# Neighbourhood attention inside a hybrid block: from one grid row of queries to tiles of 4 rows by 16 columns, with key spans of 32 columns

## The chip, the cores and the metric

The kernel runs on one core of one Trainium2 chip. The metric is the device time of one execution in microseconds. Three runs of the kernel before took 4218.52, 4212.82 and 4217.05 us; their median, 4217.05 us, is the time before.

## The reference

The program is a chain of blocks: a first block with three branches (neighbourhood attention, gated linear attention, RWKV), an output projection, windowed attention, mixture of experts, a linear recurrence and mixture of experts again. Only the neighbourhood attention of the first block changes. It works on 16 meta tokens and a grid of 16 rows by 64 columns of tokens, in 8 heads of 64. Each query sees the 16 meta tokens and a window of 8 rows by 16 columns, clipped at the grid's border, with a bias by the relative position:

```python
def row_block(r):
    rs = jnp.clip(r - wr // 2, 0, rows - wr)          # wr = 8
    kw = kb[:, :, :, col_idx]                         # 16 columns for each query column
    s_loc = jnp.einsum('bhcd,bhrckd->bhcrk', qr, kw) * scale + bias
    s_meta = jnp.einsum('bhcd,bhmd->bhcm', qr, km_h) * scale
    p = jax.nn.softmax(jnp.concatenate([s_loc, s_meta], axis=-1), axis=-1)
    return p_loc @ vw + p_meta @ vm_h                 # the result is gated by silu(g)
```

## The kernel before, in words

The attention branch is one stage between two barriers of all engines. It goes over four pairs of heads (`p` = 0 to 3; two heads of 64 fill 128 partitions). For each pair TensorE projects V, K, Q and the gate G from the normed input `hnT` (1088 columns), eight matmuls (`project_tensor`, L409) to each span of 336, 384, 320 or 512 columns, into banks 6 and 7 in turn. ScalarE copies each span out (`span_scalar`, L508 and L511). V is then turned by 16 transposes in four groups (`turn_tensor`, L422 and L425), and ScalarE copies each group (`turn_scalar`, L516 and L519).

V, K and Q of the first pair and three of the gates are projected ahead. After that a loop takes 64 items, one for each pair and each grid row `r`, in a software pipeline written out by hand. In iteration `i` TensorE issues the values matmuls of item `i-3`, half of the fill, the transposes of item `i-2`, the other half of the fill, and the scores of item `i`. The fill is the projection of the next pair's V, K and Q: 4 matmuls in each iteration, 2 in each half. In the last pair it is one matmul of the last gate in each iteration.

One item is 64 queries of two heads, 128 partitions in all:

- Scores (L456, L458): the window of 8 whole grid rows, 512 keys, and 16 meta keys in a second bank. For each head one matmul with 64 rows and 64 columns of the array.
- VectorE: meta scores scaled (L605), their maximum (L607), scores plus bias and mask with their maximum (L609), the negative (L614), and later the reciprocal of the sum (L595) and the probabilities scaled by it (L597). The keys outside the 16 columns are masked with -1e30.
- ScalarE: Exp with the sum (L561).
- TensorE: four transposes of 128 keys and one of 16 (L465, L466). ScalarE copies the four (L555), VectorE the fifth (L601).
- TensorE: values (L476, L478), five matmuls for each head. VectorE multiplies the result by the gate into `oT` (L589; in the last pair a plain copy, L591).

Three items are under way at once, each with two banks: `scores_tensor` waits for `o_taken` of the item three before. The bias comes by 8 DMAs on SyncE's queue (L359), and one VectorE instruction (L575) scales it and adds the mask that GpSimd builds. GpSimd also clears a corner of a weight buffer for the next stage (L324) once V of the last pair is projected. SyncE's queue holds the weight blocks, the bias after the fourth block, and the stores of `oT`.

A float32 matmul is two records of LDWEIGHTS and two of MATMUL in the trace; a transpose is one of each.

Of the kernel before, what the change touches and what calls it, by code (L numbers as in the profile page):

```python
# [13 lines left out]
P = 128  # L14
# [251 lines left out]
def attention_branch(k, c, ps, io, hnT, mix, sb):  # L266
# [6 lines left out]
    with stage(k, sb) as st:  # L273
        NP, NR, RING = BW // P, SEQ // CH, 4
        n = NP * NR
        wb = k.first + [st.sb(f"w_block{i}", [P, KD, P]) for i in range(2, RING)]
        ahead, low = [t.now() for t in k.first_in], st.sem("gla_low_cleared")
        qT, kT = [st.sb(f"na_q{x}", [P, SEQ]) for x in range(2)], [st.sb(f"na_k{x}", [P, COLS]) for x in range(2)]
        vT, vt = st.sb("na_v", [P, COLS]), [st.sb(f"na_v_tiles{x}", [P, NC, P]) for x in range(2)]
        gate = st.sb("na_gate", [P, NP, SEQ])  # L280
        bias = st.sb("na_bias", [P, NP * RPB_R, CH])
        away, edge = st.sb("na_outside", [P, CH]), st.sb("na_edge", [P, 2, CH])
# [4 lines left out]
        g, bias_in, biased = st.sem("na_setup"), st.sem("na_bias_in"), st.sem("na_biased")  # L287
        w_in = [st.sem(f"na_w_in{i}") for i in range(RING)]
# [4 lines left out]
        p_turned, p_copied, pm_copied, pv, o_taken, finished = (st.sem(name) for name in (  # L293
            "p_turned", "p_copied", "pm_copied", "pv", "o_taken", "finished"))
# [12 lines left out]
        turns_before = lambda s: 4 * sum(s > at[K, p][1] for p in range(NP))  # L307
# [5 lines left out]
        def turn_bank(p, i):  # L313
            return ps[6 + (at[K, p][1] + 1 + 4 * p + i) % 2]

        def spans_done(b):

            kind, p = blocks[b]
            return at[kind, p][1] + len(span_of[kind])

# [5 lines left out]
        def setup_gpsimd(gp):  # L326
            def select(ap, fill, base, pattern, part):
                gp.wait_ge(*g.now())
                gp.affine_select(out=ap, in_=ap, compare_op=ALU.is_ge, fill=fill, base=base, pattern=pattern,
                                 channel_multiplier=part).then_inc(*g.up())  # L330

            for h in HALF:
                gp.wait_ge(*g.now())
                gp.memset(away[h, :], 0.0).then_inc(*g.up())
                for base, col, q in ((WIN_C // 2, 1, -1), (WIN_C // 2 - 1, -1, 1)):
                    select(away[h, :], NEG, base + (CH - 1) * q, [[col, CH]], -q)
                for e, (base, q) in enumerate(((WIN_C // 2 - 1, -1), (-(CH - WIN_C // 2), 1))):
                    gp.wait_ge(*g.now())
                    gp.memset(edge[h, e, :], 1.0).then_inc(*g.up())
                    select(edge[h, e, :], 0.0, base + (CH - 1) * q, [[0, CH]], -q)  # L340
                    select(edge[h, e, :], 0.0, (WIN_C - 1) if e == 0 else -(CH - WIN_C),
                           [[-1 if e == 0 else 1, CH]], 0)
            gp.wait_ge(*g.now())
            gp.tensor_tensor(edge[:, 0, :], edge[:, 0, :], edge[:, 1, :], ALU.add).then_inc(*g.up())
            gp.wait_ge(*g.now())
            gp.tensor_scalar(edge[:, 0, :], edge[:, 0, :], -1.0, 1.0, ALU.mult, ALU.add).then_inc(*g.up())
            gp.wait_ge(*g.now())
            gp.tensor_tensor(away[:, :], away[:, :], edge[:, 0, :], ALU.mult).then_inc(*g.up())

        def window(r):  # L350
            first = min(max(r - WIN_R // 2, 0), NC - WIN_R)
            return first, first - r + WIN_R - 1

        def load_bias(sp):
            rpb = bass.AP(io["rpb_padded"].tensor, RPB_PAD + WIN_C - 1 - (CH - 1),
                          [[RPB_R * RPB_C, BW // 64], [1, CH], [RPB_C, RPB_R], [1, CH]])
            for h in range(2):
                for p in range(NP):
                    sp.dma_start(bias[HALF[h], p * RPB_R:(p + 1) * RPB_R, :], rpb[2 * p + h]).then_inc(*bias_in.up(16))  # L359

        def store(sp, p):
            if p < NP - 1:
                sp.wait_ge(o_taken.sem, NR * (p + 1))
# [23 lines left out]
        def span_free(pe, s):  # L387

            for p in range(NP):
                i = s - at[K, p][1] - 1  # L390
                if 0 <= i < 2:
                    pe.wait_ge(vcopied.sem, 5 * p + (3, 5)[i])
                    return
            if s >= 2:
                pe.wait_ge(copied.sem, s - 1)
# [18 lines left out]
        def turn_tensor(pe, p, i):  # L414

            pe.wait_ge(copied.sem, at[V, p][1] + 3)
            if i < 2:
                pe.wait_ge(copied.sem, at[K, p][1] + i)
            else:
                pe.wait_ge(vcopied.sem, 5 * p + i - 1)  # L420
            for j in range(4 * i, min(4 * i + 4, NC - 1)):
                x = pe.transpose(turn_bank(p, i)[:, (j % 4) * P:(j % 4 + 1) * P], vT[:, X0 + CH * j:X0 + CH * j + P],  # L422
                                 c["ident"][:, :])
            if i == 3:
                x = pe.transpose(turn_bank(p, i)[0:META, 3 * P:], vT[:, M0:X0], c["ident"][:, :])  # L425
            x.then_inc(*vturned.up())

        def fill_tensor(pe, p, r, part):

# [3448 lines left out]
```

## Time and profile before

| | us |
|---|---|
| median of 3 runs | 4217.05 |
| the profiled execution's own time | 4214.0 |
| its span | 4212.3 |
| mean granted TensorE clock, share of full | 0.979 |
| the attention stage's first matmul to the next stage's first matmul, from the timeline | 30.07 to 446.89 |
| its loop's first scores to its last ones | 119.96 to 432.57 |

Time between the stage's two ends is time of the whole kernel, since barriers of all engines stand on both sides. TensorE's busy time in the profile is a sum of records whose ends are modelled; where work follows work, the distance between two starts is the better measure.

### The profile page before, as it was taken

Reading aid. Unit: us, or ns where it says so; the run is one execution under the profiler, and the core shown is the slowest. Engines: PE = TensorE matmul, PEld = TensorE weight load, DVE = VectorE, ACT = ScalarE, POOL = GpSimd, SP = SyncE. Lnnn points to the kernel's source line nnn. Section 1 sums busy time; section 2 is a strip of 40 time slices with the busy share of each in tenths; the row PEclk is TensorE's granted clock in tenths of the full one; section 3 lists DMA queues with packets and bytes.
Section 4 is the critical chain, followed back from the end, with each engine's and each line's share of the span. In section 5 each row is a group of like instructions: output and inputs, shape, how many; then the busy total and the mean of one; then the engine's idle time right before and its main releaser. Section 6 shows DMA issues by size and latency. Waiting matters only on the chain. (4 is left out here: it accounts for less than half of the span.)

```text
span 4212.3 us, 65895 instructions
## 1 busy us (share of the span) xinstructions
PE 4009.1 (95%) x28648; PEld 2243.9 (53%) x28648; DVE 1549.1 (37%) x3413; ACT 1058.6 (25%) x2123; POOL 270.7 (6%) x342
## 2 busy tenths in 40 slices
PE   8999999999999989999998999999899998999998
PEld 4555675586868664554544444444444454444443
DVE  2344233445454541124657311111455649111113
ACT  2333221343334320104552000001245321000003
POOL 0000000101111100000110000000000100000000
PEclk9999999999999999999998999999999998999999
DMA  3000101100000013221008899999311129899997
GB/s 100 26 26 7 51 17 41 31 4 26 4 27 9 17 46 108 63 40 31 1 1 320 295 329 308 328 313 312 127 34 45 50 103 328 297 319 319 314 323 247
DMA packets 315088, 566.97 MB, mean 135 GB/s; under 512 B 48001, under 2 KB 121889, under 8 KB 314801
## 3 DMA queue, kind: packets, MB, share of 16 engines
q1 hardware_dynamic: 299328, 505.61, 35.1%
q0 software_dynamic: 9504, 34.61, 3.4%
q10 hardware_dynamic: 5968, 22.55, 1.4%
q8 instruction: 226, 3.70, 0.4%
q14 instruction: 62, 0.50, 0.0%
HBM read 514.46 MB, written 48.23 MB: 134 GB/s over the span
## 5 line engine op out<-in xcount | busy, mean ns | idle before, releaser
L3364 PE MATMUL bank<-ring,m_picked_T 128*128 128x512 f32 x2048 | 897.1, 596 | 4.1 <-ACT m_picked_T L3447 4.1
L3364 PEld LDWEIGHTS bank<-ring,m_picked_T 128*128 128x128 f32 x2048 | 388.9, 191 | 481.3 <-issue 475.7
L3364 PE MATMUL bank<-ring,m_hidden_T 128*128 128x512 f32 x1024 | 455.1, 592 | 0.0
L3364 PEld LDWEIGHTS bank<-ring,m_hidden_T 128*128 128x128 f32 x1024 | 189.7, 190 | 215.3 <-issue 215.2
L3613 DVE TENSOR_TENSOR m_hidden<-m_hidden,bank 128x512 f32<-128x512 f32 x64 | 43.9, 685 | 505.1 <-ACT m_hidden L3453 505.1
L1450 PE MATMUL bank<-hnT,first_block 128*128 128x336 f32 (+3 forms) x544 | 180.4, 483 | 8.5 <-PEq L101 7.8
L3453 ACT ACTIVATE m_hidden<-bank 128x512 f32<-128x512 f32 x64 | 38.2, 597 | 538.8 <-PE bank L3364 538.8
L241 PE MATMUL bank<-xT,first_block 128*128 128x512 f32 x352 | 152.4, 593 | 2.8 <-ACT l_i L3092 1.7
L2648 PE MATMUL bank<-xT,a_weights 128*128 128x512 f32 x320 | 142.3, 595 | 0.8 <-ACT xT L2504 0.8
L1450 PEld LDWEIGHTS bank<-hnT,first_block 128*128 128x128 f32 x544 | 102.1, 193 | 67.5 <-issue 21.2
L2728 PE MATMUL bank<-a_weights,xT 128*128 128x512 f32 x256 | 126.7, 622 | 5.0 <-DMA a_weights<-in_attn_w_o 4.6
L3619 DVE COPY m_hidden_T<-bank 128x256 f32<-128x256 f32 x64 | 27.0, 422 | 276.1 <-PE bank L3357 276.1
L409 PE MATMUL bank<-hnT,first_block 128*128 128x512 f32 (+3 forms) x336 | 123.0, 507 | 1.4 <-PEq L101 1.4
L409 PE MATMUL bank<-hnT,w_block 128*128 128x512 f32 (+3 forms) x304 | 124.3, 536 | 0.0
L3457 ACT ACTIVATE m_hidden_T<-bank 128x256 f32<-128x256 f32 x64 | 24.5, 383 | 393.5 <-PE bank L3357 393.5
L3743 POOL DMA_INDIRECT y_rows<-m_ys,m_tokens x30 | 47.7, 1589 | 1113.3 <-DVE m_ys L3628 1046.3
L2101 DVE TENSOR_TENSOR rw_lane<-bank,rw_lane 128x512 f32<-128x512 f32 (+1 forms) x100 | 60.9, 609 | 145.6 <-PE bank L1632 145.6
L241 PEld LDWEIGHTS bank<-xT,first_block 128*128 128x128 f32 x352 | 66.6, 190 | 87.3 <-issue 86.1
L3044 PE MATMUL bank<-xT,l_gT 128*128 128x512 f32 x256 | 110.1, 592 | 0.8 <-ACT l_i L3092 0.8
L3030 PE MATMUL bank<-l_xc,l_wg 128*128 128x512 f32 x256 | 110.5, 592 | 0.0
L1632 PE MATMUL bank<-rw_lane 64*64 64x64 f32 x2720 | 100.7, 218 | 5.3 <-issue 5.2
L1615 PE MATMUL bank<-rw_lane 64*64 64x64 f32 x2720 | 100.3, 220 | 3.9 <-issue 2.9
(500 smaller groups left out, 6091.5 us busy)
## 6 DMA issues: line engine op xcount, KB each, us to landing
ring<-in_moe_w_gate_up SPq DMA_DIRECT2D x512, 512.0 KB, 7.6
ring<-in_moe_w_down SPq DMA_DIRECT2D x256, 512.0 KB, 4.6
first_block<-in_w_in SPq DMA_DIRECT2D x23, 512.0 KB, 3.7
w_block<-in_w_in SPq DMA_DIRECT2D x19, 512.0 KB, 3.7
x_rows<-X ACTq DMA_DIRECT2D x2, 4096.0 KB, 17.5
ring<-y_rows SPq DMA_DIRECT2D x16, 512.0 KB, 8.9
out_w<-in_w_out ACTq DMA_DIRECT2D x11, 512.0 KB, 13.6
first_block<-in_lru_w_in SPq DMA_DIRECT2D x11, 512.0 KB, 3.9
```

Source lines behind the costliest of these rows:

```text
L241: m = pe.matmul(ps[banks + j][0:out_rows, 0:n], w[:, d, 0:out_rows], src[:, d, col:col + n], start=d == 0, stop=d == KD - 1)
L409: x = pe.matmul(bank_of(s + j)[:, 0:w], wb[b % RING][:, d, :], hnT[:, d, col:col + w], start=d == 0, stop=d == KD - 1)
L1450: m = pe.matmul(banks[j][:, 0:n], wb[i % 3][:, d, :], hnT[:, d, col:col + n], start=d == 0, stop=d == KD - 1)
L1615: x = pe.matmul(L.tall(0)[B_(d), h, i, :], power_t(L, e, d, h, i), power(L, e, d, h, i))
L1632: x = pe.matmul(L.tall(2)[B_(d), h, i, :], power(L, e, d, h, i), L.TT[B_(d), h, i, :])
L2101: ve.tensor_tensor(L.part(2), L.bank[2][:, 0:2 * L.n * CH], L.part(2), ALU.add).then_inc(*tt_added.up())
L2648: x = pe.matmul(main_bank(s)[:, :], w, xT[:, d, tokens_of(s)], start=d == 0, stop=d == KD - 1)
L2728: x = pe.matmul(ps[6 + half][:, :], oT[:, b, t * P:(t + 1) * P], weights[:, b, 512 * half:512 * half + 512], start=b == 0, stop=b == KD - 1)
L3030: out = pe.matmul(ps[s % 4][:, :], wg[:, q, z, h, x * P:(x + 1) * P], xc[:, h, col:col + w], start=h == 0, stop=h == 1)
L3044: out = pe.matmul(ps[2 * (t % 4) + h][:, :], gT[:, b, t * P:(t + 1) * P], wo[:, b, 512 * h:512 * h + 512], start=b == 0, stop=b == KD - 1)
L3364: m = pe.matmul(banks[j][:, :], lhsT[:, (i % 8) * P:(i % 8 + 1) * P], ring[:, i, j, :], start=i % 8 == 0, stop=i % 8 == KD - 1)
L3743: gp.indirect_dma_start(y_rows[:, :], bass.IndirectOffsetOnAxis(ap=tokens[:, e:e + 1], axis=0), ys[:, :], None, compute_op=ALU.add).then_i ...
```

## The change

An item is now a tile of 4 grid rows by 16 columns of queries, still 64 queries of two heads, and there are still 16 of them to a pair of heads. Its keys are a span of 32 columns (from column 0, 8, 24 or 32) of 9, 12, 12 or 10 lines, with the meta tokens in one of these lines: 288, 384, 384 or 320 keys in a single bank. Items are handled two at a time, so that the loop has 32 steps; a step's half of the fill is four matmuls (one in the last pair). The bias arrives as 12 by 48 values for each query, by 32 DMAs of 16 partitions. GpSimd cuts twelve "images" from it for each pair (bias plus mask, for three kinds of tile and four row blocks) during the loop. The masks are built on 32 partitions, turned by four transposes in bank 0 and copied by VectorE. V is kept four times, once for each column window, which makes five groups of four transposes. Queries are stored tile by tile.

```diff
-        s_sb, pT, stat = ([st.sb(f"na_{name}{u}", shape) for u in range(3)] for name, shape in (
-            ("scores", [P, 512 + META]), ("probs_T", [P, 5, P]), ("stats", [P, 6])))
+        FIRST, LONG, META_LINE = (0, 0, 4, 8), (9, 12, 12, 10), (4, 4, 0, 9)
+        vT, vt = st.sb("na_v", [P, 4, V_LINES, WIDE]), [st.sb(f"na_v_tiles{x}", [P, 4, 5, P]) for x in range(2)]
+        s_sb = [st.sb(f"na_scores{u}", [P, 3 * P]) for u in range(6)]
+        pT = [st.sb(f"na_probs_T{u}", [P, 3, P]) for u in range(6)]
...
+        def images_gpsimd(gp):
+            gp.wait_ge(mask_in.sem, 1)
+            gp.wait_ge(biased.sem, 1)
+            for p, rb in ((p, rb) for p in range(NP) for rb in range(4)):
+                if p:
+                    gp.wait_ge(maxed.sem, STEPS * (p - 1) + 2 * rb + 2)
...
+                    for x in range(3):
+                        for line, row, count in ROWS[rb]:
+                            gp.tensor_tensor(image[f][rb][:, x, line:line + count, :], rows[...],
+                                             mask[:, x, :].unsqueeze(1).broadcast_to([P, count, WIDE]), ALU.add)
...
-            for h in HALF:
-                pe.matmul(a[h, :], qT[p % 2][h, CH * r:CH * r + CH], kT[p % 2][h, first:first + 512])
-            for h in HALF:
-                x = pe.matmul(b[h, 0:META], qT[p % 2][h, CH * r:CH * r + CH], kT[p % 2][h, M0:X0])
+            if t >= 3:
+                pe.wait_ge(o_taken.sem, 2 * (t - 2))
+            for i in (2 * t, 2 * t + 1):
+                for h in range(2):
+                    x = pe.matmul(bank(i)[half(i, h), 0:LONG[rb] * WIDE].rearrange("p (r c) -> p r c", c=WIDE),
+                                  qT[p % 2][HALF[h], queries], lines(kT[p % 2], FIRST[rb], LONG[rb], w)[HALF[h]])
...
-            for j in range(4):
-                pe.transpose(a[:, j * P:(j + 1) * P], s_sb[u][:, j * P:(j + 1) * P], c["ident"][:, :])
-            pe.transpose(b[0:META, P:2 * P], s_sb[u][:, 512:512 + META], c["ident"][:, :]).then_inc(*p_turned.up())
+            for j in range(3):
+                keys = P if j < 2 else tail(rb)
+                x = pe.transpose(bank(i)[0:keys, j * P:(j + 1) * P], s_sb[i % 6][:, j * P:j * P + keys], c["ident"][:, :])
...
+            for j in range(3):
+                keys = P if j < 2 else tail(rb)
+                for h in range(2):
+                    x = pe.matmul(bank(i)[HALF[h], 3 * P:3 * P + CH], vt[p % 2][0:keys, w, FIRST[rb] // 4 + j, HALF[h]],
+                                  pT[i % 6][0:keys, j, half(i, h)], start=j == 0, stop=j == 2)
...
+            for t in range(steps + 3):
+                if t >= 3:
+                    for i in (2 * t - 6, 2 * t - 5):
+                        values_tensor(pe, i)
+                if t < steps:
+                    fill_tensor(pe, t, 0)
+                if 2 <= t < steps + 2:
+                    for i in (2 * t - 4, 2 * t - 3):
+                        turn_probs_tensor(pe, i)
+                if t < steps:
+                    fill_tensor(pe, t, 1)
+                    scores_tensor(pe, t)
...
-                    ve.tensor_scalar(s_sb[u][:, 512:], b[:, 0:META], scale, None, ALU.mult).then_inc(*chain.up())
-                    ve.tensor_reduce(stat[u][:, 0:1], s_sb[u][:, 512:], AX.X, ALU.max).then_inc(*chain.up())
+                    for i in (2 * t, 2 * t + 1):
+                        ve.tensor_tensor_reduce(
+                            s_sb[i % 6][:, 0:w], bank(i)[:, 0:w], image[0][rb][:, x, :, :].rearrange("p r c -> p (r c)"),
+                            scale, lowest[:, 0:1], ALU.add, ALU.max, stat[u][:, 0, i % 2:i % 2 + 1]).then_inc(*chain.up())
```

In `span_scalar` the V span is now copied once for each of the four windows (20 instructions to a pair instead of 3), the K span into lines with the meta tokens twice (6 instead of 3), and each Q span in two pieces. ScalarE copies the probabilities of an item in two pieces, 256 columns and the tail; VectorE's copy of the fifth is gone. GpSimd's clearing of the weight corner comes after all images in its order.

## Rows read from the trace of the kernel before

**Rows 1.** The page: its first line and the engines' busy time.

```profile
span 4212.3 us, 65895 instructions
PE 4009.1 (95%) x28648; PEld 2243.9 (53%) x28648; DVE 1549.1 (37%) x3413; ACT 1058.6 (25%) x2123; POOL 270.7 (6%) x342
```

**Rows 2.** Stretches of the stage: PE, PEld, DVE, ACT, POOL busy, then PEclk, DMA.

```profile
120.00:208.00 88.00, 87.61 (x659) 51.63 (x659) 37.19 (x147) 28.60 (x61) 0.00 (x0) 1.00 0.08 22
385.00:440.00 55.00, 52.55 (x538) 30.32 (x535) 32.86 (x133) 21.72 (x48) 0.00 (x0) 0.98 0.06 13
...
382.50:410.58 28.08, 28.08 (x281) 15.94 (x280) 17.89 (x73) 10.46 (x25) 0.00 (x0) 1.00 0.11 25
```

**Rows 3.** Waits in the stage: who waited for whom, us in total, times, longest.

```profile
PEld bank L456 <- DVE na_oT L591: 9.9, 13, 0.8
...
PEld bank L476 <- ACT na_probs_T L555: 3.1, 2, 2.0
...
PE bank L476 <- DVE na_probs_T L601: 1.8, 1, 1.8
```

**Rows 4.** Timeline of TensorE, one row of the last pair: start us, us, engine.

```profile
382.50 1.07 PE L456 MATMUL bank<-na_k,na_q 64*64 64x512 f32 x4
...
383.41 0.24 PE L458 MATMUL bank<-na_k,na_q 64*64 64x16 f32 x4
...
383.58 0.69 PE L476 MATMUL bank<-na_probs_T,na_v_tiles 128*64 128x64 f32 x16
...
384.20 0.33 PE L478 MATMUL bank<-na_probs_T,na_v_tiles 16*64 16x64 f32 x4
...
384.46 0.66 PE L465 MATMUL bank<-ident,na_scores 128*128 128x128 f32 x4
...
385.06 1.02 PE L409 MATMUL bank<-hnT,w_block 128*128 128x512 f32 x2
...
386.02 1.08 PE L456 MATMUL bank<-na_k,na_q 64*64 64x512 f32 x4
```

**Rows 5.** The same view in an earlier pair: half a fill, then scores.

```profile
192.35 1.88 PE L409 MATMUL bank<-hnT,first_block 128*128 128x512 f32 x4
194.16 1.08 PE L456 MATMUL bank<-na_k,na_q 64*64 64x512 f32 x4
```

**Rows 6.** Timeline where V is turned, pair 1: TensorE and ScalarE.

```profile
152.72 0.60 PE L422 MATMUL bank<-ident,na_v 128*128 128x128 f32 x4
152.92 0.45 ACT L511 ACTIVATE na_k<-bank 128x336 f32<-128x336 f32 x1 [0.54 <-PE bank L409]
153.36 0.60 ACT L516 ACTIVATE na_v_tiles<-bank 128x512 f32<-128x512 f32 x1
...
153.52 1.21 PE L422 MATMUL bank<-ident,na_v 128*128 128x128 f32 x8 [0.20 <-ACT na_k L511]
...
155.48 1.08 PE L456 MATMUL bank<-na_k,na_q 64*64 64x512 f32 x4
```

**Rows 7.** Groups by shape, VectorE and ScalarE: busy us, mean ns, idle before.

```profile
L609 DVE CUSTOM_DVE_ANT_0 na_scores<-bank,na_bias,na_stats 128x512 f32<-128x512 f32 x64 | 48.1, 751 | 2.3
L561 ACT ACTIVATE na_scores<-na_scores,na_stats 128x528 f32<-128x528 f32 x64 | 47.1, 735 | 159.0 <-DVE na_stats L614 159.0
...
L597 DVE TENSOR_SCALAR na_scores<-na_scores,na_stats 128x528 f32<-128x528 f32 x64 | 31.7, 495 | 2.2
...
L519 ACT ACTIVATE na_v_tiles<-bank 16x128 f32<-16x128 f32 x4 | 1.0, 249 | 0.0
```

**Rows 8.** GpSimd's groups by shape, a sum of two tiles elsewhere.

```profile
L3211 POOL TENSOR_TENSOR l_r<-l_r 128x1024 f32<-128x1024 f32 x8 | 26.6, 3324 | 351.8 <-DVE l_r L3180 351.8
```

**Rows 9.** Timeline of the bias: its DMA issues and its VectorE instruction.

```profile
31.07 12.61 SPq L359 DMA_DIRECT2D na_bias<-in_rpb_padded  x8
...
47.66 4.16 DVE L575 SCALAR_TENSOR_TENSOR na_bias<-na_bias,na_outside 128x3840 f32<-128x3840 f32 x1 [18.24 <-DMA na_bias<-in_rpb_padded]
```

**Rows 10.** Stretches after the last fill, columns as in rows 2.

```profile
434.20:438.50 4.30, 1.88 (x27) 1.25 (x25) 1.51 (x7) 1.91 (x5) 0.00 (x0) 0.90 0.02 4
438.50:440.20 1.70, 1.53 (x20) 1.23 (x20) 0.09 (x1) 1.69 (x2) 0.00 (x0) 0.50 0.00 0
446.80:451.30 4.50, 4.41 (x8) 1.65 (x9) 0.00 (x0) 1.28 (x1) 3.39 (x11) 0.51 0.77 240
```

More of the change, by code:

```diff
@@ L306, in attention_branch, with taken @@
             at[kind, p] = (b, sum(len(span_of[x]) for x, _ in blocks[:b]))
-        turns_before = lambda s: 4 * sum(s > at[K, p][1] for p in range(NP))
+        turns_before = lambda s: 5 * sum(s > at[K, p][1] for p in range(NP))
+        kind_of = [kind for kind, _ in blocks for _ in span_of[kind]]
+        def taken(s):
+            by_vector = kind_of[s] == G
+            return (gated if by_vector else copied).sem, sum((x == G) == by_vector for x in kind_of[:s + 1])
         def bank_of(s):
@@ L319, in spans_done, with item, half, bank @@
             return at[kind, p][1] + len(span_of[kind])
+        def item(i):
+            return i // TILES, i % TILES // 4, i % 4
+        def half(i, h):
+            return HALF[h]
+        def bank(i):
+            return ps[2 * (i // 2 % 3) + i % 2]
+        def lines(t, first, count, w):
+            return t[:, first * CH:(first + count) * CH].rearrange("p (r c) -> p r c", c=CH)[:, :, WINDOW[w]:WINDOW[w] + WIDE]
+        def tail(rb):
+            return LONG[rb] * WIDE - 2 * P
         def clear_low_gpsimd(gp):
@@ L354, in load_bias, with select @@
-        def load_bias(sp):
[L355 to L359, printed above, removed]
+            def select(ap, base, part, h, r, q):
+                gp.wait_ge(*mask_built.now())
+                gp.affine_select(out=ap, in_=ap, compare_op=ALU.is_ge, fill=NEG, base=base,
+                                 pattern=[[0, h], [r, 4], [q, ap.shape[3]]], channel_multiplier=part).then_inc(*mask_built.up())
@@ new lines, in setup_gpsimd @@
+            for line in META_LINES:
+                for t in kT:
+                    gp.memset(t[:, line * CH:line * CH + CH], 0.0).then_inc(*cleared.up())
+                gp.memset(vT[:, :, line:V_LINES if line > 4 else line + 1, :], 0.0).then_inc(*cleared.up())
+            gp.memset(maskT[:, :, :], 0.0).then_inc(*mask_built.up())
+            by_query = [maskT[0:WIDE, x, :].rearrange("p (h y q) -> p h y q", h=2, y=4) for x in range(4)]
+            near, far = slice(0, 8), slice(8, 16)
+            select(by_query[0][:, :, :, :], -7, 1, 2, 0, 1)
@@ new lines, in setup_gpsimd @@
+            select(by_query[0][:, :, :, near], 22, -1, 2, 0, -1)
+            select(by_query[0][:, :, :, far], 15, -1, 2, 0, 0)
+            select(by_query[1][:, :, :, :], -15, 1, 2, 0, 1)
+            select(by_query[1][:, :, :, :], 30, -1, 2, 0, -1)
+            select(by_query[2][:, :, :, near], -16, 1, 2, 0, 0)
+            select(by_query[2][:, :, :, far], -15, 1, 2, 0, 1)
+            select(by_query[2][:, :, :, far], 30, -1, 2, 0, -1)
+            select(by_query[3][:, :, :, :], -3, 1, 2, 1, 0)
@@ L468, in values_tensor @@
+            x.then_inc(*p_turned.up())
         def values_tensor(pe, i):
[L469 to L479 removed]
@@ L482, in tensor, with turn_masks_tensor @@
+            x.then_inc(*pv.up())
+        def turn_masks_tensor(pe):
+            pe.wait_ge(*mask_built.now())
+            for x in range(4):
+                y = pe.transpose(ps[0][:, x * P:(x + 1) * P], maskT[:, x, :], c["ident"][:, :])
+            y.then_inc(*mask_turned.up())
         def tensor(pe):
@@ L484, in tensor @@
             project_tensor(pe, K, 0, 0, 8)
-            for i in range(4):
+            turn_masks_tensor(pe)
+            for i in range(5):
                 turn_tensor(pe, 0, i)
@@ L542, in scalar @@
             span_scalar(ac, K, 0, 0)
-            for i in range(4):
+            for i in range(5):
                 turn_scalar(ac, 0, i)
```

330 lines of the change are left out of this document (179 added, 151 removed).

## The prediction

> **What bounds the kernel now.** I read the page's head first. TensorE is busy 95% of the span, no other engine over 37% [rows 1]. That is a mean over stages, and this change touches one stage only, so next came the stretches of that stage. In the loop TensorE is busy 87.6 of 88.0 us at a granted clock of 1.00 (its 2.4 GHz level), VectorE 37, ScalarE 29; in the last pair VectorE comes to 33 of 55 [rows 2]. Then the waits: what TensorE's two sequencers wait for in the loop is small, 9.9, 3.1 and 1.8 us in total [rows 3], and the first of these is a weight load that waits beside matmuls still streaming: eight rows of the last pair take 28.08 us and TensorE is busy for all of them [rows 2]. So the loop goes at the pace of TensorE's instruction stream, and each microsecond taken out of that stream is one off the kernel, as long as no other chain takes over.
>
> **What a row costs today.** Distances between starts in one row of the last pair [rows 4]: scores 0.91, meta scores 0.17, values 0.62 for 16 records, meta values 0.26 for 4, five transposes 0.60, one matmul of fill 0.96; together 3.52 us. Without the fill it is 2.56 us, and 64 rows pay that. A half fill in the earlier pairs is four records in 1.81 us [rows 5]; at 0.43 us each (0.86 for two of them in the row above) about 0.10 of it is the step from one kind of work to the next. The scores' four records take 0.91 and not 1.71 us: the two heads stream side by side in their quarters of the array, and the change keeps that pairing.
>
> **What a tile will cost.**
> - Scores: widths 288, 384, 384, 320, mean 344 in place of 512. 0.86 x 344/512 + 0.05 = 0.62 us. The 16 meta keys ride in a spare line, so their 0.17 is gone.
> - Values: 12 records in place of 20. The eight on 128 keys take 8 x 0.039 = 0.31. The last four have 128 keys in half of the tiles (0.155) and 32 or 64 in the other half. No row has 32 or 64; the nearest has 16 and takes 0.26, and I take that. Mean 0.21, and 0.05 for the step to the next kind: 0.57.
> - Transposes: 3 in place of 5, 0.60 x 3/5 = 0.36.
>
> Sum 1.55 against 2.56: 1.01 less, x64 = **-64.6 us**. The four meta-value records in rows 4 cost 0.065 each where the 16 before them cost 0.039. The Trainium skill (TensorEngine Tiling (Array Packing), Key Properties) says that a change of tiling mode drains TensorE; the trace agrees as far as such a pair of rows can show it. By that rule the step back to 128 keys for the second tile of a pair costs the same 0.10 again in half of the tiles, 3.3 us in all, and the sum at the end would be -60.3 in place of -63.6.
>
> **Fewer segments.** In the first three pairs the fill comes in 48 pieces instead of 96: 48 x 0.10 = **-4.8 us**. The last pair keeps its 16.
>
> **Turning V.** This one is on the path. Today it takes 2.76 us between the last matmul of the K span and the next scores [rows 6], most of it TensorE waiting for ScalarE: 0.45 for the K copy before the second group, then copies of 0.60 in turn with the transposes. There will be five groups, and the K span is copied in four pieces (32, 32, 256 and 64 wide, near 1.0 us by the 0.60 for 512 and 0.25 for 128 [rows 6, 7]). So 0.55 more before group two and 0.6 for another group: +1.2 us, four times, **+4.8 us**. Between 0 (all behind other work) and twice that. The mask's four transposes (about 0.45) come before the first pair's turning and fit into its wait for the K copy.
>
> **The drain** after the last scores is a chain, not a stream: two reductions, two Exps, two scalings, then transposes, copies and values for two tiles at a time. It takes two tiles where one row stood, but each is shorter; I step it through with the durations below and get 11 us from last scores to the last product, against about 10.4 now. **+1.0 us**, between -1 and +4.
>
> **What I cost at nothing, and its cover.**
> - VectorE, each pair: two reductions of 0.60 (0.75 for 512 wide, 344 now), two scalings of 0.40 (0.495 for 528 wide), outputs 0.43, reciprocal and negative 0.31 [rows 7]: 2.9 us. TensorE's pair lasts 2 x 1.55 + 2 x 0.96 = 5.0 in the last pair of heads, 7.7 to 10 before. Were that cover gone it would be the bound.
> - ScalarE, each pair: two Exps near 0.68 (0.735 for 528 wide, and reading out the sum), copies of 0.38 and 0.28 for each tile: 2.7 us. The V span's twelve pieces (about 3 us) and the five turn copies (3 us) fall in steps of 7.7 us and more.
> - GpSimd, images: 4,700 elements for each pair of heads at no more than 3.2 ns [rows 8] is 15 us, 17 with the small ones. The first is ready near 70 us, wanted at 120; each later one has eight steps, some 60 us, and asks about 5. The mask (11 selects and fills of 0.2 to 0.4) starts at 30 and is wanted at 50.
> - The bias: 6,144 pieces of 192 bytes in place of 7,680 of 256. Its issue holds SyncE's queue for 12.6 us today, 1.6 for each DMA [rows 9]. With 32 DMAs it lies between the same 12.6 (by pieces) and 50 (by DMA); the weights queued behind are wanted at 90 us, so at 50 it ends at 81 and is still hidden. VectorE's scaling shrinks from 4.2 us to about 2, but stands ahead of the gates in its queue: past 88 us it would hold TensorE up through the gate's banks.
> - The clearing of the weight corner, now behind the images, comes at the end of pair 3 of 4; SyncE's store of that pair goes ahead of it anyway.
>
> **Sum:** -64.6 - 4.8 + 4.8 + 1.0 = **-63.6 us**. The profiled execution's own time is 4214.0 (span 4212.3 and 1.7 around it), which gives 4150.4. The median of the runs shown is 3 us higher, 4217.05, which gives 4153.4. I take 4152, between them.
>
> **Rivals.**
> 1. *A chain takes over in the last pair of heads.* From scores: 0.15, reductions 1.25, negative 0.2, Exps 1.3, then in ScalarE's order the copies of the pair before, 1.3, 0.15 to TensorE, and there the rest of a step, 4.4: 8.8 us for two steps, against 10.0 of TensorE's stream. The slack is 1.2. If copies or reductions on these cut-up operands take half as much again, a step becomes 6 us: 8 x 1.0 = 8 more, and about 4160. Against it: 1.2 us of slack. For it: nothing in the trace shows such operands. Chance 0.10.
> 2. *The clock falls where V is turned.* The trace shows the clock at 0.50 from 438.5 us, after 4.3 us in which TensorE was busy for 1.9, and again at 0.51 for the 4.5 us after the barrier [rows 10]. The turning will last 4 us, with TensorE busy for 2.6. If the clock falls each time, work at full clock of some 2.2 us is lost four times: +9, 4161. Against it: no fall at 2.8 us today, and more work in each. Chance 0.08.
> 3. *Strided keys stream slowly.* Score matmuls read 32 columns, skip 32. If that halved the rate, +0.57 x 64 = 37: 4189. No row of this stage shows it; pieces of 32 floats are long. Chance 0.05.
> 4. *The quarters or the shared weight loads save more than I count*, or the small key tails cost nothing extra: 128-key records throughout and no turning penalty give -72, 4144. Chance 0.10.
> 5. *Slower.* The place is the loop itself: two tiles' short work in a row is thinner than long streams, and if the clock stood at 1.2 GHz where it now stands at 2.4, the loop (313 us now, about 247 then) would pay for it. The point from which it decides: a loss of 64 us, a quarter of the new loop run as 64 more. At half of the loop it is +124, 4276. Against it: 1.00 throughout a loop of which a third is such short work, and the long projection's share of it rises. Chance 0.03.
>
> That the change doesn't do what it says would show as fewer keys saved; the widths are plain in the code, and I give it nothing beyond rival 4.
>
> **Numbers.** The sum of my own case carries 0.64; its own range, from the bounds of turning, drain and key tails, is 4144 to 4160. The range for 8 in 10 takes in the first two rivals and the fourth in part: 4140 to 4165. A measurement of this kernel can tell about 0.2%, 8 us, from no change; every case but the slow one is beyond it, and of that one's 0.03 I put 0.01 inside it. Faster 0.97, same 0.01, slower 0.02.
>
> **What would show it.** In the profile after: score records 288 to 384 wide and starts 1.2 us apart for a pair of tiles; 24 value records in about 1.1 us; six transposes in 0.7; a period of 5.0 us for a pair in the last heads with TensorE busy throughout; the first scores near 121 and the next stage's first matmul near 383. Wrong would be: TensorE waiting on `o_taken`, on the tail copies or on the bias; a granted clock under 1.00 in the loop; score records longer than 0.75 of the old ones; a turning of more than 5 us.

## The result, and the profile after

The changed kernel takes **4150.43 us** (median of four runs, 4148.62 to 4152.04); the kernel before, run beside it, takes 4215.26 (four runs, 4212.82 to 4218.52). The ratio is 0.9846, with a 95% interval of 0.9829 to 0.9863. The forecast was 4152 us in 4140 to 4165. The profiled execution took 4149.54 us, its span 4147.5: 64.5 less than the profiled execution before, where the sum said 63.6.

The page's first line and busy times, against [rows 1]:

```profile
span 4147.5 us, 64228 instructions
PE 3944.2 (95%) x27772; PEld 2204.1 (53%) x27772; DVE 1485.6 (36%) x3158; ACT 1051.5 (25%) x2275; POOL 324.3 (8%) x436
```

TensorE is busy for 65 us less, and the span is 65 us shorter: the gain came out of TensorE's stream. GpSimd has 54 us more, the images and the mask, and nobody waits for them.

Where it came from is read by stage. The stage goes from its first matmul to the next stage's first one. Before, that was 30.07 to 446.89, 416.8 us; now it is 30.84 to 381.04, 350.2 us: **66.6 less**. It began 0.8 later, and the untouched rest of the program took 1.4 more in this execution. Inside it, first scores to last scores went from 311.7 to 241.6 us (called *the loop* below). The 432.57 that the table of the kernel before gives for its last scores is the start of the last meta scores; the last scores themselves start at 431.66:

```profile
431.66 1.08 PE L456 MATMUL bank<-na_k,na_q 64*64 64x512 f32 x4
```

So the stage's 66.6 us are 70.1 less in the loop, 3.3 more before its first scores and 0.2 more after its last ones.

The stretches, with the columns of [rows 2]: the loop, six pairs of tiles in the last heads, the second turning of V, two pieces of the drain, the start of the next stage:

```profile
120.00:200.00 80.00, 79.29 (x467) 46.51 (x465) 23.76 (x87) 30.92 (x117) 13.33 (x20) 1.00 0.10 27
335.68:365.60 29.92, 29.92 (x254) 15.89 (x253) 14.33 (x60) 12.72 (x48) 0.00 (x0) 1.00 0.11 24
144.80:148.28 3.48, 2.77 (x22) 2.04 (x20) 0.00 (x0) 2.64 (x8) 0.00 (x0) 1.00 0.00 0
367.00:370.00 3.00, 1.54 (x30) 1.21 (x28) 1.87 (x9) 1.68 (x7) 0.00 (x0) 1.00 0.00 0
372.00:375.00 3.00, 2.39 (x27) 1.63 (x24) 0.40 (x3) 2.97 (x7) 0.00 (x0) 0.61 0.00 0
381.00:385.50 4.50, 4.46 (x8) 1.66 (x9) 0.00 (x0) 1.28 (x1) 3.40 (x11) 0.50 0.75 237
```

In the last heads TensorE is busy 29.92 of 29.92 us, and VectorE and ScalarE less than half of it. The clock stands at 1.00 in the loop and in the turning; it drops only in the drain and after the barrier, as in [rows 10].

TensorE's timeline in the last heads, one whole step (a pair of tiles) and the start of the next, then the values of a later step. In a step the kernel issues scores, values, fill, transposes and fill. It answers to [rows 4]:

```profile
335.68 1.19 PE L528 MATMUL bank<-na_k,na_q 64*64 64x288 f32 x8
336.79 1.36 PE L548 MATMUL bank<-na_probs_T,na_v_tiles 128*64 128x64 f32 x24
338.08 1.12 PE L484 MATMUL bank<-hnT,w_block 128*128 128x512 f32 x2
339.04 0.82 PE L537 MATMUL bank<-ident,na_scores 128*128 128x128 f32 x6
339.70 1.02 PE L484 MATMUL bank<-hnT,w_block 128*128 128x512 f32 x2
340.65 1.51 PE L528 MATMUL bank<-na_k,na_q 64*64 64x384 f32 x8
342.09 1.35 PE L548 MATMUL bank<-na_probs_T,na_v_tiles 128*64 128x64 f32 x24
...
351.24 1.51 PE L528 MATMUL bank<-na_k,na_q 64*64 64x384 f32 x8
352.68 0.92 PE L548 MATMUL bank<-na_probs_T,na_v_tiles 128*64 128x64 f32 x24
353.52 1.13 PE L484 MATMUL bank<-hnT,w_block 128*128 128x512 f32 x2
```

Read the distances between starts. Scores take 1.11 us at 288 columns and 1.44 at 384. Values take 1.28 in the step at 336.79 and 0.84 in the one at 352.68, with the same 24 records: the first pair's last four records of each tile read 32 or 64 keys, the second's read 128. Transposes take 0.66, the two pieces of fill 0.96 each. The six steps of the stretch above come to 4.99 us each, for 5.0 forecast. Over the four kinds of pair, scores come to 1.305 us (288: 1.12, 320: 1.22, 384: 1.44, twice), values to 1.065, transposes to 0.65: 3.02 for a pair of tiles, **1.51 for a tile**, where the forecast said 1.55.

The earlier heads, against [rows 5], where half a fill took 1.81 us:

```profile
166.75 3.70 PE L484 MATMUL bank<-hnT,first_block 128*128 128x512 f32 x8
170.28 0.82 PE L537 MATMUL bank<-ident,na_scores 128*128 128x128 f32 x6
```

Eight records in a piece take 3.53 us; two pieces of four took 3.62.

The second turning of V, against [rows 6]; the bracket is the idle time before a record and who ended it:

```profile
144.80 0.60 PE L497 MATMUL bank<-ident,na_v 128*128 128x128 f32 x4
...
145.82 1.12 PE L497 MATMUL bank<-ident,na_v 128*128 128x128 f32 x8 [0.42 <-ACT na_k L600]
...
147.23 1.12 PE L497 MATMUL bank<-ident,na_v 128*128 128x128 f32 x8 [0.29 <-ACT na_v_tiles L622]
148.28 1.51 PE L528 MATMUL bank<-na_k,na_q 64*64 64x384 f32 x8
```

It lasts 3.48 us, 0.72 more than before; TensorE still waits for ScalarE twice. The third and fourth last the same. The first lasts 3.40, with the mask's four transposes (0.44) ahead of it: 3.83 in all, where it was 2.78.

TensorE's waits in the stage, against [rows 3]:

```profile
PEld bank L548 <- ACT na_probs_T L658: 2.4, 2, 1.8
...
PE bank L548 <- ACT na_probs_T L660: 1.9, 2, 1.5
```

Both are the drain's. The 9.9 us behind `na_oT` are gone from the list.

### The profile page after: what moved, and what is told of

The parts are those of the page before. It is cut to its first block and busy times, and to the rows that moved or that the text cites. A ratio compares the mean times of both kernels' runs of the same rounds, so it can differ in the third digit from the quotient of the medians.

```text
span 4147.5 us, 64228 instructions
## 1 busy us (share of the span) xinstructions
PE 3944.2 (95%) x27772; PEld 2204.1 (53%) x27772; DVE 1485.6 (36%) x3158; ACT 1051.5 (25%) x2275; POOL 324.3 (8%) x436
## 5 line engine op out<-in xcount | busy, mean ns | idle before, releaser
L241 PEld LDWEIGHTS bank<-xT,first_block 128*128 128x128 f32 x352 | 66.6, 190 | 87.1 <-issue 86.1
L1725 PE MATMUL bank<-rw_lane 64*64 64x64 f32 x2720 | 100.9, 220 | 6.6 <-issue 5.5
L2037 ACT ACTIVATE rw_lane<-bank 128x512 f32<-128x512 f32 (+1 forms) x100 | 53.3, 533 | 199.3 <-PE bank L1725 198.6
```

The source lines that it names most:

```text
L241: m = pe.matmul(ps[banks + j][0:out_rows, 0:n], w[:, d, 0:out_rows], src[:, d, col:col + n], start=d == 0, stop=d == KD - 1)
L1725: x = pe.matmul(L.tall(0)[B_(d), h, i, :], power_t(L, e, d, h, i), power(L, e, d, h, i))
L2037: ac.activation(L.M[e % 2], L.tall(0), ACT.Copy).then_inc(*m_copied.up())
```

## The experiments

The last rows give the theory: **A**, TensorE's instruction stream still sets the pace, and what a step costs is read from its rows. Against it stood that the chain through VectorE and ScalarE was already close to taking over; that strided keys or the short tails cost something else than A said; and that the sum was right by errors that cancel. Eleven runs followed, each beside the kernel before. Whole times scatter by some microseconds in stages that no kernel here touches. The stretch from the stage's first matmul to the first scores scatters by up to 2.7 us (91.5 in reduce_twice, 94.2 in keys_in_a_row), with the moment at which the granted clock rises from 0.50 to 1.00 there. So the loop is compared as well: the changed kernel's is 241.56 us, and when the same file ran a second time it was 241.55.

**The changed kernel again** (no edit), as a measure of that scatter.

> The changed kernel once more, on the same chip as the two that follow: loop 241.56 us and stage 350 us as in its first profile (within 1 us, for the clock's rise at the stage's start), time within 0.2% of 4150. Theory and rivals say the same here.

Measured 4151.88 us (six runs, 4147.82 to 4160.32), ratio 0.9845 [0.9832, 0.9858], stage 350.15.

### What the short tails cost

**All tails read as 128 keys.** The last piece of transposes, copies and values has 128 keys in every tile. GpSimd clears the buffers once, at the start; after that, what lies past the real keys is left over from the wider tiles that used the same buffer. So this kernel prices TensorE's stream but does not compute the branch: it leaves out whatever would keep those weights at zero.

```
-                keys = P if j < 2 else tail(rb)
+                keys = P
```

> The changed kernel with the last piece of keys 128 wide in every tile, for transposes, copies and values (the scores stay as narrow as they are, so what stands behind the 32 or 64 real keys is left over from other tiles: the softmax's weights there are not the reference's). In the changed kernel 24 value records of two tiles take 1.28 us where the last piece has 32 or 64 keys and 0.85 us where it has 128. Theory A, a change of the tile size in the array costs time: all 32 pairs of tiles take 0.85, 16 of them lose 0.43 us, 6.9 us in all, so 4143.5 against 4150.4, and the two steps of such tiles in the last heads shorten from 4.98 to 4.55 us. Theory B, these tiles are slow for another reason (their place at the grid's edge, what streams before them): the records stay at 1.28 and the time at 4150.

Measured 4145.48 us (4143.93 to 4146.85), ratio 0.9833 [0.9816, 0.9849]; loop 235.45. Its TensorE timeline, in a step whose tiles have narrow tails in the changed kernel:

```profile
332.78 0.92 PE L550 MATMUL bank<-na_probs_T,na_v_tiles 128*64 128x64 f32 x24
333.63 1.12 PE L486 MATMUL bank<-hnT,w_block 128*128 128x512 f32 x2
```

More arithmetic takes less time: 0.85 us for the values in every step. That is 0.43 less in each narrow step, and 14 of those values lie inside the loop: 6.0 us, and the loop lost 6.11. In TensorE's stream, reading fewer keys is a loss here. What it would cost to keep the extra weights at zero, no run priced.

**Narrow tails last.** What is it in a narrow tail that costs: that it is narrow, or that the array goes back to 128 keys for the second tile? Here both tiles' 128-key pieces come first, then both tails.

```
+            for js in ((0, 1), (2,)):
+                for i in (i0, i0 + 1):
...
+                    for j in js:
+                        keys = P if j < 2 else tail(rb)
```

> The changed kernel with the values matmuls of two tiles in another order: both tiles' pieces of 128 keys first, then both last pieces. The array's tile size then changes twice for a pair of tiles instead of four times. Theory A, each change costs about 0.11 us: 16 pairs of tiles save 0.2 us each, 3.4 us in all, 4147.0. Theory B, each narrow matmul is slow by itself, whatever stands before it: nothing changes, 4150.4.

Measured 4148.32 us (4143.26 to 4151.95), ratio 0.9839 [0.9823, 0.9856]; loop 237.46, 4.10 less. Its TensorE timeline, narrow tails again:

```profile
333.03 1.06 PE L550 MATMUL bank<-na_probs_T,na_v_tiles 128*64 128x64 f32 x24
334.02 1.12 PE L484 MATMUL bank<-hnT,w_block 128*128 128x512 f32 x2
```

Values take 0.99 in place of 1.28. The same 24 records in another order save 0.29 a step, x14 = 4.1. So of the 0.43, 0.29 is the way from narrow to 128 keys and back to narrow, and 0.14 what one turn to narrow still costs. Steps whose tails have 128 keys anyway take 0.85 in either order, so it isn't the new order as such that saves.

### The steps between kinds of work

**Fill in four pieces.** The fill of a step is cut in four again, values and transposes done tile by tile as before the change.

```
+                for u in range(2):
+                    if t >= 3:
+                        values_tensor(pe, 2 * t - 6 + u)
+                    if t < steps:
+                        fill_tensor(pe, t, 2 * u)
```

> The changed kernel with the fill of the first three pairs of heads cut into four pieces for each step, as many for each tile as there were for each row before, and values and transposes issued tile by tile. Theory A, a piece of fill pays 0.10 us for the step from short work to long: 48 more pieces, +4.8 us, 4155. Theory B, that 0.10 belongs to the tile and not to the piece: no change, 4150.4.

Measured 4158.41 us (4156.01 to 4165.17), ratio 0.9866 [0.985, 0.9883]; loop 249.54, **7.98 more**, not 4.8. Its TensorE timeline in early heads:

```profile
166.92 1.98 PE L484 MATMUL bank<-hnT,first_block 128*128 128x512 f32 x4
168.74 0.49 PE L538 MATMUL bank<-ident,na_scores 128*128 128x128 f32 x3
169.07 1.88 PE L484 MATMUL bank<-hnT,first_block 128*128 128x512 f32 x4
170.88 0.57 PE L549 MATMUL bank<-na_probs_T,na_v_tiles 128*64 128x64 f32 x12
171.38 1.98 PE L484 MATMUL bank<-hnT,first_block 128*128 128x512 f32 x4
```

Four records of fill take 1.82 and 1.81: two pieces 3.63 against 3.53, so 0.10 for a piece, as forecast. What I had left out is that the values are entered twice as well: one tile's 12 values on 128 keys take 0.50, two tiles' 24 in one go 0.85. With x for twelve records and e for entering, x + e = 0.50 and 2x + e = 0.85: x is 0.35 (0.029 for a record) and e 0.15. The same two numbers give 0.61 for 16 records, and [rows 4] show 0.62. In steps with narrow tails the values cost no more than before, 2 x 0.64 for 1.28. In the last heads, where values now follow right behind the transposes, a tile's transposes take 0.42 and not 0.33. Step by step the timeline gives 21 x 0.20 for the fill, 15 x 0.15 for the values and 8 x 0.19 for the transposes: 7.97 of the 7.98.

The 0.10 isn't paid by every piece, though. In one step of this kernel there are no values yet, and a piece of fill stands between two transposes. First it, then eight such records of the changed kernel between scores and transposes:

```profile
132.92 2.32 PE L484 MATMUL bank<-hnT,w_block 128*128 128x320 f32 x8
```

```profile
131.64 2.42 PE L484 MATMUL bank<-hnT,w_block 128*128 128x320 f32 x8
```

From start to start they take 2.16 and 2.26. Next to transposes, which use the whole array as the fill does, a piece pays nothing; the 0.10 belongs to the border with scores or values, which use a part of its columns or rows. The changed kernel agrees: of the two equal pieces in the step that turns V, the one next to values takes 2.36 (139.52 to 141.88) and the one between two kinds of transposes 2.26 (142.54 to 144.80). Otherwise each piece of fill has one such border, which is why counting pieces worked.

**The kernel before without its meta keys.** This leaves out the 16 meta tokens: their scores, transpose, copy and values, and VectorE's work for them.

```
-            for h in HALF:
-                x = pe.matmul(b[h, 0:META], qT[p % 2][h, CH * r:CH * r + CH], kT[p % 2][h, M0:X0])
...
-            for j in range(5):
+            for j in range(4):
```

> The kernel before, with the meta keys left out (no meta scores, no fifth transpose, no meta values, none of VectorE's work for them; the output lacks the meta tokens in this branch). It asks whether starts in the timeline price work rightly. By them a row pays 0.17 for meta scores, 0.26 for meta values and 0.12 for the fifth transpose: 0.55 us. Theory A: a row of the last pair falls from 3.51 to 2.96, the loop from 312.61 by 0.55 x 62.5 = 34 to 278, the time to 4182. Theory B, TensorE's small work is hidden by something and another chain sets the row: less than half of that, above 4200.

Measured 4190.53 us (4185.95 to 4195.16), ratio 0.994 [0.9925, 0.9955]; loop 284.38. Against 311.7 that is 27.3 less and not 34. One row of its last heads:

```profile
355.76 1.08 PE L456 MATMUL bank<-na_k,na_q 64*64 64x512 f32 x4
356.77 0.69 PE L472 MATMUL bank<-na_probs_T,na_v_tiles 128*64 128x64 f32 x16
357.38 0.66 PE L463 MATMUL bank<-ident,na_scores 128*128 128x128 f32 x4
357.88 1.02 PE L409 MATMUL bank<-hnT,w_block 128*128 128x512 f32 x2
358.83 1.08 PE L456 MATMUL bank<-na_k,na_q 64*64 64x512 f32 x4
```

The row takes 3.07 us, 0.44 less and not 0.55 (62 x 0.44 is 27.3). Scores now last 1.01 where [rows 4] show 0.91 with the same records: 0.10 of the 0.17 that stood on the meta scores stays when they go. The step that it most likely belongs to is the one from the scores' quarters on 64 rows to values on 128. So a visit to scores costs 0.15 beyond the 0.86 of its streams. The changed kernel pays that once for a pair of tiles, 2 x 0.86 x 344/512 + 0.15 = 1.31; the 1.24 forecast had 0.05 for each tile, 0.10 for a pair.

### Strided keys

**Keys in a row.** The score matmuls read as many columns, but side by side and not 32 of every 64 (so other keys are scored).

```
-            return t[:, first * CH:(first + count) * CH].rearrange("p (r c) -> p r c", c=CH)[:, :, WINDOW[w]:WINDOW[w] + WIDE]
+            return t[:, first * CH:first * CH + count * WIDE].rearrange("p (r c) -> p r c", c=WIDE)
```

> The changed kernel with the scores' keys read from consecutive columns instead of 32 of every 64 (as many of them, but the wrong ones: the scores are not the reference's). Theory A, the stride costs TensorE nothing: scores of two tiles of 384 keys stay at 1.44 us and the time at 4150.4. Theory B, the 0.06 us by which they stand over my 1.38 is the stride's: 1.38, and 2 us less in all, 4148. Under the third rival of the prediction (half rate) it would have been 37 us less; the changed kernel's own rows speak against that already.

Measured 4149.19 us (4147.27 to 4153.04), ratio 0.9845 [0.9829, 0.9862]; loop 241.56, to the hundredth what it was. Skipping every other 32 columns costs nothing. Rival 3 is out.

### How much cover is left

**Each reduction twice,** then **three times** (the instruction of line 719, one after another on VectorE; the second kernel has `range(2)`).

```
+                        for _ in range(1):
+                            ve.wait_ge(*chain.now())
+                            ve.tensor_tensor_reduce(
...
```

> The changed kernel with each VectorE reduction of scores done twice (same result). That adds near 1.4 us to the chain from scores to probabilities in each step. In the last heads ScalarE's copies end 1.5 us before TensorE wants them. Theory A, TensorE's stream is the bound everywhere: nothing changes, loop 241.6 us. Theory B, the chain already binds in the last heads: each of their steps grows by up to 0.7 us, loop near 246.

Measured 4156.04 us (4153.35 to 4156.93), ratio 0.9855 [0.9838, 0.9873]. The loop grew by 0.43 us only (241.99), with about 1.2 us more of VectorE in each of 32 steps; last scores to the next stage, which nothing hides, grew from 15.44 to 17.68. Three of the last heads' steps make the 0.43 (0.10, 0.06 and 0.28), so the cover is nearly used up. The stage as a whole took 351.18, with a start 1.7 shorter; the rest of the difference lies outside it.

> The same with each reduction done three times: 2.8 us more on the chain, 1.3 beyond the slack of 1.5. The chain spans two steps, so under theory A each step of the last heads grows by some 0.65 us, 4 to 5 us in all, and those of the first three pairs, 7.4 to 10 us long, not at all: loop 246. Under theory B (the chain binds already) it is 9 to 10 us, loop 251.

Measured 4165.15 us (4161.27 to 4169.66), ratio 0.988 [0.9861, 0.9899]; loop 249.68, 8.1 more, not 4 to 5. Its TensorE timeline and waits:

```profile
349.02 1.51 PE L528 MATMUL bank<-na_k,na_q 64*64 64x384 f32 x8 [0.63 <-DVE na_oT L687]
```

```profile
PEld bank L528 <- DVE na_oT L687: 8.3, 5, 1.9
...
PE bank L528 <- DVE na_oT L687: 4.1, 5, 1.1
```

This step of the last heads lasts 6.0 us (343.03 to 349.02) in place of 5.3. The scores wait for the bank that VectorE's output copy frees, and that copy stands in VectorE's own queue behind the reductions. VectorE isn't busy throughout: 4.82 us of these 5.99, and most of the rest is one wait for ScalarE's Exps. First that wait, then VectorE's wait for scores in the changed kernel:

```profile
343.93 0.17 DVE L706 RECIPROCAL na_stats<-na_stats 128x2 f32<-128x2 f32 x1 [0.96 <-ACT na_scores L666]
```

```profile
347.61 0.62 DVE L719 CUSTOM_DVE_ANT_0 na_scores<-bank,na_bias_image,na_lowest 128x384 f32<-128x384 f32 x1 [1.60 <-PE bank L528]
```

So what takes over is not the chain of rival 1, which goes through TensorE and spans two steps, but a shorter round within one step: VectorE's reductions, ScalarE's Exps, VectorE's scalings, and the next reductions behind them in its queue. The 1.60 us is its slack in the changed kernel in this step, enough for about 1.2 us of reductions more and not for 2.4. The last eight steps grew by 0.4 to 1.4 each, 8.1 together; all earlier ones, which are longer, kept their length even with the third reduction.

**Images built once.** GpSimd builds the bias images of the first pair of heads only; later pairs reuse them (so they get the first pair's bias). It tests whether its work beside VectorE's costs time.

```
-            for p, rb in ((p, rb) for p in range(NP) for rb in range(4)):
+            for p, rb in ((0, rb) for rb in range(4)):
```

> The changed kernel with GpSimd cutting the bias images of the first pair of heads only; the other three pairs use them too, so their bias is that of the first pair. Theory A, the images are off the path and only VectorE feels them: the loop from first to last scores stays at 241.56 us and the time at 4150; VectorE's scaling of 384-wide probabilities, which takes 554 ns on the mean in the changed kernel and between 360 and 1248, falls to near 375 for all once GpSimd is idle. Theory B, images hold the loop up somewhere: 241.56 shrinks. Under A with no link between the two engines, the scaling's mean stays at 554.

Measured 4153.06 us (4151.51 to 4157.1), ratio 0.9853 [0.9835, 0.987]; loop 241.56, the same. VectorE's groups (mean ns behind the comma) in the changed kernel, then in this one:

```profile
L710 DVE TENSOR_SCALAR na_scores<-na_scores,na_stats 128x384 f32<-128x384 f32 x32 | 16.4, 554 | 0.6
```

```profile
L710 DVE TENSOR_SCALAR na_scores<-na_scores,na_stats 128x384 f32<-128x384 f32 x32 | 12.0, 417 | 0.6
```

The mean of these scalings is 554 ns in the changed kernel and 417 here. It is the mean of two kinds: in the changed kernel's trace 12 of the 32 overlap a GpSimd instruction and take 784 ns in the mean, the other 20 take 416. A scaling 320 wide took up to 1248 ns, and none of any width took over 422 here. The reductions, 615 ns in both kernels, say nothing of such a link, since none of them overlapped a GpSimd instruction in either. VectorE has the slack, so the loop doesn't notice.

### Can the turning be hidden?

**Turning spread.** The five groups that turn V stand apart in TensorE's order: the first where all five were, one behind the scores, two between the values, the last behind the transposes of a step.

```
             if lo == 28:
-                for i in range(5):
-                    turn_tensor(pe, p + 1, i)
+                turn_tensor(pe, p + 1, 0)
```

> The changed kernel with the five groups of V's transposes of pairs 2 to 4 no longer in a row: the first stays behind the K span, the second comes after the scores, two more between the values of the next step, the fifth after its transposes. The turning takes 3.48 us at one place in the changed kernel, 2.2 of it TensorE's own work. Theory A, the other 1.3 us are waiting for ScalarE's copies, and go: three times, -3.8 us, loop 237.8. Theory B, spreading them costs TensorE a step between kinds of work at each place, 0.1 us and more, five times: about -2, loop 239.5.

Measured 4153.49 us (4151.94 to 4156.9), ratio 0.9849 [0.9833, 0.9866]; loop 238.94, 2.62 less: between what the two theories said (the whole time stands no lower than the changed kernel's; the stage, 347.58, does). Its TensorE timeline, a group between other work:

```profile
146.66 0.66 PE L497 MATMUL bank<-ident,na_v 128*128 128x128 f32 x4
147.24 0.71 PE L547 MATMUL bank<-na_probs_T,na_v_tiles 128*64 128x64 f32 x12
```

The waits are gone, but such a group next to values or scores costs 0.58 us, where eight transposes in one go take 1.05 from start to start. The values are entered twice, which costs nothing here (2 x 0.64, their tails being narrow).

**Both:** narrow tails last and the turning spread; it computes what the changed kernel computes. The diff is that of the two together, except that no group can stand between the values of two tiles any more: one now comes ahead of them and one behind.

> The changed kernel with two edits together: the narrow pieces of two tiles last in the values, and V's transposes spread. Apart they took 4.10 and 2.62 us off the loop. Theory A, TensorE's stream is still the bound: the sum, loop 234.8 us, and the time 6.7 us under the changed kernel's. Theory B, with the stream that much shorter (a step of edge tiles in the last heads falls from 4.98 to 4.69 us) the chain through VectorE and ScalarE takes over: loop above 236.

Measured 4147.16 us (six runs, 4135.4 to 4149.84), ratio 0.9827 [0.9813, 0.984]; loop 235.71, 5.85 less, where the parts add up to 6.72. The trace has a new wait, three times, 0.7 us in all, for most of the missing 0.87:

```profile
152.04 0.63 PE L497 MATMUL bank<-ident,na_v 128*128 128x128 f32 x4 [0.23 <-ACT na_v_tiles L635]
```

The stage takes 344.87 us, 5.3 less, and the median is 4.7 below that of the changed kernel on the same chip (0.1%). The intervals of the two ratios overlap, so as whole times the runs don't separate them; the stage does.

## Why the prediction held, step by step

| Step | Forecast, us | Measured, us |
|---|---|---|
| tiles in place of rows, 64 | -64.6 | -64.8 |
| 48 fewer pieces of fill | -4.8 | -4.8 |
| turning V, four times | +4.8 | +3.2 |
| drain | +1.0 | +0.4 |
| sum | -63.6 | -66.0 (stage: -66.6) |

The table's sum is 0.6 short of the stage's. Of that, 0.4 lies behind VectorE's last product: 3.8 us to the next stage before, 3.4 now.

**What bounds the kernel:** right. TensorE was busy for every moment of the last heads before and after, and each edit in its stream moved the loop by what its rows said (wide_tails 6.0 and 6.1, tails_last 4.1 and 4.1), while work taken from GpSimd moved it by nothing.

**The tile:** the difference was right, and in part by luck. Measured is 48 rows at 2.51 us (transposes took 0.55 in the early heads, not 0.60) and 16 at 2.56, less 32 pairs at 3.02. So I had the old rows 2.4 us too dear in all, and the new pairs, at 3.10, 2.6 too dear; that the two cancel is chance.
- *Scores,* 1.24 a pair said, 1.305 measured. A visit costs 0.15 and not 2 x 0.05: I took out the meta scores' whole 0.17, of which 0.10 stays (no_meta), and charged 0.05 for each tile, which a pair pays once.
- *Values,* 1.14 said, 1.065 measured, by two misses that cancel. A pair on 128 keys takes 0.85, not 2 x 0.515 = 1.03: I paid for entering at every tile, and a pair enters once. A narrow pair takes 1.28; I said 1.24, because narrow tails cost 0.43 more than wide ones and not the 0.21 that I had taken.
- *Transposes,* 0.72 said, 0.65 measured.

The step back to 128 keys, weighed and left out of the sum, belonged in it: with it the difference would have been 0.41, and tails_last shows that the detour from narrow to wide and back alone is 0.29. The sum came out right without it because every pair had been charged for entering a second time, which wide_tails and four_pieces show in the values' rows: 0.18 too much in a wide pair, and in a narrow one 0.16 once the step back is counted. The Trainium skill (TensorEngine Tiling (Array Packing), Key Properties) says that a change of tiling mode, and not just of tile, drains TensorE. The runs here agree, with 0.29 us for such a detour, 0.10 at each border of fill with scores or values, and nothing at its border with transposes.

**Fewer segments:** right in size, 3.53 us against 2 x 1.81. The 0.10 is the price of a border with scores or values and not of a piece as such, as four_pieces shows; in the two kernels compared here the count is the same.

**Turning V:** right in mechanism and sign, a third too large. The term that was too large is K's copy in four pieces: it took 0.68 us (145.00 to 145.68), not near 1.0. The second group starts 1.02 us after the first (144.80 to 145.82) where it was 0.80, so 0.22 more and not 0.55, and the fifth group added 0.50 of the 0.6 said. The first turning itself took 3.40, but the mask's transposes ahead of it, which I had fitted into its wait, added their 0.44 and saved it only 0.08.

**The drain:** last scores' end to VectorE's last product (443.10 before, 377.64 now) went from 10.4 to 10.8.

**What was costed at nothing** stayed free, except for the mask's transposes. The bias took 17.0 us to issue, near the lower of my bounds (12.6 and 50):

```profile
31.84 17.00 SPq L434 DMA_DIRECT2D na_bias<-in_rpb_padded  x32
```

The next weights were issued behind it, at 48.88. VectorE's pair was priced too low (scaling 0.40 said, 0.51 measured in the mean, by the GpSimd work beside it), but reduce_twice shows 1.2 us more of it hidden almost whole.

**The rivals.** 1, the chain of the last heads: no, and reduce_thrice shows that the shorter round of VectorE and ScalarE would bind first. 2, the clock where V is turned: 1.00 there. 3: no, by keys_in_a_row. 4, more saved: the result lies 1.6 us under the forecast, but not by its mechanism, since small tails cost more and not nothing. 5, a clock of 1.2 GHz in the loop: it stood at 1.00 there.

**Signs that were wrong.** The first scores stand at 124.04, not 121. Counted from the stage's first matmul they come 3.3 us later than before. Step 0 now puts eight fill matmuls ahead of them where there were four: from the first turning's end to the first scores it took 66.83 us and takes 69.09, 2.26 more. The first turning, with the mask's transposes, grew by 1.05. The fill is moved work, and the loop is shorter by it. The next stage's first matmul stands at 381.04, not 383.

**What stays open:** why the untouched stages differ by some microseconds between executions; no run looked into them.

## What to carry to other kernels

Where one engine is busy without a gap, add up the distances between starts in its timeline, and price apart what a kind of work costs to enter and what each record of it adds; an average of a row hides both. Group work of one shape: here TensorE goes through 128 keys for all tails faster than through fewer, because a narrow piece between wide ones costs more than it saves. Whether padding pays in the end depends on what keeps the padded weights at zero, which no run here had to do; putting the narrow pieces last needs nothing of the kind and got 4.1 of the 6.1 us. When a small piece of work is taken away, ask which part of its time is the step to its neighbour, since that part stays.

## What the runs showed of the hardware

- Entering 128-key values costs 0.15 us and each record 0.029 (four_pieces); a detour narrow, wide, narrow inside them costs 0.29, with narrow tails of 32 keys as with 64 (tails_last), where I had weighed 0.20 and left it out. Fill next to scores or values pays 0.10, fill next to transposes nothing (four_pieces).
- Float32 keys in runs of 32 out of 64 columns stream as fast as contiguous ones (loop 241.56 in both).
- A scaling on VectorE, 384 wide, takes 416 ns by itself and 784 in the mean where a GpSimd instruction overlaps it (12 of 32); the worst, 320 wide, took 1248. The reduction that reads a bank was never overlapped, so the runs can't say how it would fare. The Trainium skill (SBUF — State Buffer, SBUF: two separate sides) says that the two engines share one pair of ports under an exclusive lock; the runs agree in that each slowed scaling ended about 0.2 us behind the end of a GpSimd instruction (at 169.87 behind 169.66, at 170.88 behind 170.67; GpSimd's for the images take 447 to 1075 ns), but no run took the lock apart.
